# A norm between fp32 matmul stages taken in two token halves, and the units of the next stage rounded at other places

## The reference, cut to what matters

```python
def rmsnorm_2(x, g):
    xf = x.astype(jnp.float32)
    y = xf * lax.rsqrt(jnp.mean(xf * xf, axis=-1, keepdims=True) + EPS)
    return (y * g.astype(jnp.float32)).astype(x.dtype)
...
def hybrid_layer(h, p_i, pos, lb, norm_g, w_in, w_out, ffn1_gu, ffn1_down, ffn2_gu, ffn2_down,
                 hg_norm_g, sinks, sg_ln_g, sg_w, sg_b, ple_proj, ple_gate):
...
    h = h + 0.5 * rmsnorm_2(swiglu(rmsnorm_2(h, norm_g[0]), ffn1_gu, ffn1_down), norm_g[1])
    z = rmsnorm_2(h, norm_g[2]) @ w_in
...
    h = h + rmsnorm_2(mixed, norm_g[3])
    h = h + 0.5 * rmsnorm_2(swiglu(rmsnorm_2(h, norm_g[4]), ffn2_gu, ffn2_down), norm_g[5])
    gate = jax.nn.sigmoid(rmsnorm_2(h, norm_g[6]) @ ple_gate)
    h = h + rmsnorm_2((p_i @ ple_proj) * gate, norm_g[7])
    return h
```

## Time and profile before

| | us |
|---|---|
| median of three runs | 2706.15 (2705.19 to 2709.1) |
| the profiled execution | 2708.01, its span 2706.2 |
| PE busy | 2607.4 (96% of the span) |
| DVE busy | 1133.2 (42%) |
| ACT busy | 997.6 (37%) |
| POOL busy | 1261.9 (47%) |

### The profile page before, as it was taken

How to read it: one execution, slowest core, us unless ns; L and a number is a source line. 1 busy time by engine, 2 the same in 40 slices (tenths; PEclk the granted TensorE clock), 3 DMA queues, 4 the chain that set the end, 5 groups by cost and what they waited for, 6 DMA issues and landing times.

```text
span 2706.2 us, 33653 instructions
## 1 busy us (share of the span) xinstructions
PE 2607.4 (96%) x12436; PEld 2097.1 (77%) x12436; DVE 1133.2 (42%) x1712; ACT 997.6 (37%) x1482; POOL 1261.9 (47%) x1632
## 2 busy tenths in 40 slices
PE   6999999999999999999999999999999989999997
PEld 3788777787888877677888877888877767888875
DVE  5588666535221058625221046222018655222025
ACT  5233423524223244444323245323234454232234
POOL 1233467555555454135555455555544314555543
PEclk8999999999999999999999999999999999999999
DMA  6212211132333332112333322333322202333332
GB/s 269 70 55 71 79 46 40 54 118 86 101 95 94 100 92 67 35 56 85 96 99 93 102 93 80 100 94 96 99 86 84 63 24 86 93 95 100 95 96 74
DMA packets 63815, 234.24 MB, mean 87 GB/s; under 512 B 7361, under 2 KB 8001, under 8 KB 63169
## 3 DMA queue, kind: packets, MB, share of 16 engines
q1 hardware_dynamic: 61056, 222.33, 26.4%
q10 hardware_dynamic: 2624, 10.00, 1.0%
HBM read 230.00 MB, written 2.10 MB: 86 GB/s over the span
## 4 chain that ended last, share of the span: by engine, by line
PE 85%; DVE 9%; issue 3%; ACT 2%; POOL 1%; DMA 1%; SPq 0%; DVEq 0%; POOLq 0%; ACTq 0%
PE banks L1874 21%; PE banks L1864 21%; PE banks L1865 21%; PE banks L2215 2%; PE banks L2221 2%; PE banks L2216 2%; DVE tmp L1136 2%; DVE sq_sum L1115 1%; DVE xlo L1143 1%; PE banks L1934 1%; PE banks L2024 1%; PE banks L2336 1%; DVE h L1139 1%; PE banks L2285 1%; PE banks L2287 1%
## 5 line engine op out<-in xcount | busy, mean ns | idle before, releaser
L437 POOL TENSOR_TENSOR wlo<-raw,whi 128x256 fp32r<-128x256 f32 x1584 | 1181.8, 779 | 1371.9 <-ACT whi L528 1371.7
L1864 PE MATMUL banks<-xhi,whi 128*128 128x512 f32 x1920 | 752.5, 392 | 2.3 <-DVE z L1772 2.3
L1865 PE MATMUL banks<-xhi,wlo 128*128 128x512 f32 x1920 | 747.5, 389 | 0.0
L1874 PE MATMUL banks<-xlo,whi 128*128 128x512 f32 x1952 | 736.5, 393 | 10.2 <-DVE xlo L1143 10.1
L528 ACT ACTIVATE whi<-raw 128x1024 fp32r<-128x1024 f32 x396 | 415.1, 1053 | 348.3 <-PE banks L1874 337.8
L1874 PEld LDWEIGHTS banks<-xlo,whi 128*128 128x128 f32 x1952 | 365.8, 189 | 96.7 <-DVE xlo L1143 18.4
L1864 PEld LDWEIGHTS banks<-xhi,whi 128*128 128x128 f32 x1920 | 360.4, 188 | 82.0 <-DVE z L1772 3.1
L1865 PEld LDWEIGHTS banks<-xhi,wlo 128*128 128x128 f32 x1920 | 360.5, 188 | 76.5 <-issue 1.9
L1115 DVE TENSOR_TENSOR sq_sum<-sq_sum,tmp 128x512 f32<-128x512 f32 x110 | 85.3, 775 | 464.6 <-ACT tmp L548 464.6
L1864 PE MATMUL banks<-act_hi,whi 128*128 128x512 f32 x704 | 273.9, 389 | 0.0
L1865 PE MATMUL banks<-act_hi,wlo 128*128 128x512 f32 x704 | 273.9, 389 | 0.0
(11 more groups left out here) (419 smaller groups left out, 3186.8 us busy)
## 6 DMA issues: line engine op xcount, KB each, us to landing
raw<-in_stream SPq DMA_DIRECT2D x396, 512.0 KB, 3.5
ada_raw<-in_stream SPq DMA_DIRECT2D x24, 512.0 KB, 7.0
h<-in_x ACTq DMA_DIRECT2D x2, 2048.0 KB, 12.1
out<-h SPq DMA_DIRECT2D x4, 512.0 KB, 2.6
ctx_raw<-in_ctx ACTq DMA_DIRECT2D x1, 1024.0 KB, 19.6
dft_t<-in_dft_t ACTq DMA_DIRECT2D x1, 1024.0 KB, 4.8
ple_raw<-in_ple ACTq DMA_DIRECT2D x2, 512.0 KB, 3.5
mixpar<-in_mixpar ACTq DMA_DIRECT2D x2, 384.0 KB, 4.4
```

Of the source, the lines that this page charges most:

```text
L437: piece = pool.tensor_tensor(wlo[:, i, s], raw[:, i, s], whi[:, i, s].bitcast(F32), ALU.subtract)
L1864: pe.matmul(acc[acc_of[t]][:], whi[:, u % SLOTS, i], x_h, start=(k == 0), stop=False, skip_group_check=split)
L1865: pe.matmul(acc[acc_of[t]][:], wlo[:, u % SLOTS, i], x_h, start=False, stop=False, skip_group_check=split)
L1874: mm = pe.matmul(acc[acc_of[t]][:], whi[:, u % SLOTS, i], x_l, start=False, stop=(k == k_tiles - 1), skip_group_check=leading and m < leads)
```

## The change

The last tile of out1, down and out2 is computed for the tokens 0 to 255 (half A) and then for 256 to 511 (half B), in two banks (`last_tile`, `second`), with matmuls of 256 columns. The sum of the squares of the first seven tiles stands before the last k of half A, the sum of the last tile's squares of half A before k = 3 of half B, that of half B after the first eight matmuls of the next stage. The leading tiles take k = 0 to 3 (`AHEAD` = 4) for half A, then for half B, then k = 4 to 7 whole (`leading`). ACT and DVE follow the same order: norm, residual, high and low parts of k = 0 to 3 in halves. ACT's units of the next stage are rounded at other places, and more of them by the end of the boundary (`norm_in`, `y_out`). The sum of h's squares moves out of the leading tiles: to the start of tile 5, in in2 to k = 2 of tile 4. DVE's additions of h's squares all move behind k = 4, the last four to the end. After proj both halves of the inverse come first (`at_once`) and the last tile is whole; the last boundary of all is in halves for k < 4 too. A weight unit of a split last tile is released by half B. The load of `ple_raw` moves from before to after `norm_in`.

In all 680 matmuls of 512 columns become 1360 of 256: 48 in out1, 66 in each of four downs, 24 in each of two out2s, and 40 in each of eight leading groups.

The diff, cut:

```diff
+AHEAD = 4
...
+                bank.append(0 if m == n - 1 else m % 4)
...
+            if (name == "out1" or name[0] in ("down", "out2")) and m == n - 1:
+                second[t] = 1 if name == "out1" else bank[t - 1]
+                earlier_second[t] = last[second[t]]
+                last[second[t]] = t
...
+            def norm_in(q, gain):
+
+                at_once = q[1] == 0 and q[0]
+                last_square(0)
+                if at_once:
+                    last_square(1)
+                last_inverse(0)
+                if at_once:
+                    last_inverse(1)
+                high_parts(units_to(q) + 1)
                 for e in range(2):
-                    dst = inv_rms[:, e * HALF:e * HALF + HALF]
-                    act.wait_ge(*after("summed", (key, e)))
-                    act.activation(dst, bank[4 + e][:, 0:HALF], ACT.Ln, scale=1.0 / D, bias=eps).then_inc(*done("log", (key, e)))
-                    act.wait_ge(*after("log", (key, e)))
-                    act.activation(dst, dst, ACT.Exp, scale=-0.5).then_inc(*done("inverse", (key, e)))
-
-            def norm_in(q, gain):
-
-                high_parts(units_to(q) + SLOTS - 1)
-                for k in range(KT):
-                    if k == 2:
+                    if e and not at_once:
+                        last_square(1)
+                        high_parts(units_to(q) + SLOTS)
+                        last_inverse(1)
+                    for k in range(AHEAD):
+                        act.wait_ge(*after("h_new", (q, k, e)))
+                        act.activation(xhi[:, k, half(e)], h[:, k, half(e)], ACT.Copy, scale=gain[:, k:k + 1])\
+                            .then_inc(*done("x_high", (q, k, e)))
+                        if e == 0 and k == 1:
+                            high_parts(units_to(q) + SLOTS - 1)
+                if last_copy:
+                    last_copy.pop()()
+                for k in range(AHEAD, KT):
+                    if k == AHEAD:
                         high_parts(units_to(q) + SLOTS)
                     if k == 5:
                         high_parts(units_to(q) + SLOTS + 1)
+                    if k == KT - 1:
+                        high_parts(units_to(q) + SLOTS + 2)
+                    act.wait_ge(*after("h_new", (q, k)))
+                    act.activation(xhi[:, k], h[:, k], ACT.Copy, scale=gain[:, k:k + 1])\
+                        .then_inc(*done("x_high", (q, k)))
+                    squares("h_sq", q, k - AHEAD, h[:, k - AHEAD])
+                for k in range(KT - AHEAD, KT):
                     squares("h_sq", q, k, h[:, k])
...
-                for m in range(KT):
+                for m in range(KT - 1):
+                    if m == KT - 2:
+                        high_parts(first_block[stage] // UNIT + KT * k // UNIT + (stage[0] == "out2"))
                     tile_ready(stage, m, k)
                     t = first_tile[stage] + m
                     squares("y_sq", q, m, acc[acc_of[t]][:])
-                    if m < KT - 1:
+                    act.activation(y[:, m], acc[acc_of[t]][:], ACT.Copy).then_inc(*done("y_copied", (q, m), bank_of=t))
+                t = first_tile[stage] + KT - 1
+                if stage[0] == "out2":
+                    high_parts(first_block[stage] // UNIT + KT * k // UNIT + 2)
...
+                for e in range(2):
+                    v.wait_ge(*after("inverse", (post, e)))
+                    for k in range(AHEAD):
+                        renewed(k, half(e), (q_pre, k - 1, e) if k else None, [(q_pre, k, e)] + [(q_pre, k)] * e)
+                        if e == 0 and k == AHEAD - 1 and between:
+                            between()
+                        if k and q_pre != "last":
+                            lower(k - 1, half(e), (q_pre, k - 1, e))
+                    if q_pre != "last":
+                        lower(AHEAD - 1, half(e), (q_pre, AHEAD - 1, e))
+                for k in range(AHEAD, KT + 1):
+                    if k < KT:
+                        renewed(k, slice(0, SEQ), (q_pre, k - 1), [(q_pre, k)])
+                    if k > AHEAD and q_pre != "last":
+                        lower(k - 1, slice(0, SEQ), (q_pre, k - 1))
+                        sq_add("h_sq", q_pre, k - 1 - AHEAD)
+                for k in range(KT - AHEAD, KT) if q_pre != "last" else []:
+                    sq_add("h_sq", q_pre, k)
...
+                m, t = KT - 1, first_tile[stage] + KT - 1
+                for e in range(2):
+                    freed = earlier_second[t] if e else earlier[t]
+                    if counted and freed is not None:
+                        pe.wait_ge(*bank_free(freed))
+                    for k in range(k_tiles):
+                        if e == 0 and k == k_tiles - 1:
+                            first_squares()
+                        if e and k == when:
+                            sum_half(0)
+                        u, i = place(stage, m, k, k_tiles, leads)
+                        if e == 0 and (i == 0 or k == 0):
+                            pe.wait_ge(unit_split, u + 1 - WHOLE_UNITS)
+                        dst, w_h, w_l = last_half(t, e), whi[:, u % SLOTS, i], wlo[:, u % SLOTS, i]
+                        pe.matmul(dst, w_h, hi(k)[:, half(e)], start=(k == 0), stop=False)
+                        pe.matmul(dst, w_l, hi(k)[:, half(e)], start=False, stop=False)
+                        mm = pe.matmul(dst, w_h, lo(k)[:, half(e)], start=False, stop=(k == k_tiles - 1))
+                        keys = [("unit", u)] * (e and i == UNIT - 1) + [(stage, m, e)] * (k == k_tiles - 1)
+                        if keys:
+                            mm.then_inc(*done("product", *keys))
...
+            def leading(stage, key, sum_half):
+
+
+                for e in range(2):
+                    for k in range(AHEAD):
+                        leading_high(stage, key, k, e)
+                        if e == 0 and k == 0 and sum_half:
+                            sum_half(1)
+                        if k:
+                            leading_low(stage, key, k - 1, e)
+                    leading_low(stage, key, AHEAD - 1, e)
+                for k in range(AHEAD, KT):
+                    leading_high(stage, key, k)
+                    if k > AHEAD:
+                        leading_low(stage, key, k - 1)
+                leading_low(stage, key, KT - 1)
+
+            def tile_of(stage, m, k_tiles, leads, hi, lo, waits=None, amid=None):
+
...
+                    stage = (("gu", layer, 0), ("in2", layer), ("gu", layer, 1), ("gate", layer))[s]
+                    leading(stage, lambda k: (q, k), sum_half)
+                    amid = ((LEADS, 2) if s == 1 else (LEADS + 1, 0)), lambda: pre_sum(q)
+                    y_squares = lambda: first_squares("y_sq", q)
+                    sum_half = lambda e, q=q: last_squares(("post", q), "y_sq", q, e)
...
```

316 lines of the change are left out of this document (175 added, 141 removed).

## The result

The changed kernel takes 2720.26 us (median, 2718.26 to 2722.16), the kernel before beside it 2706.73: a ratio of 1.0044 with an interval of 1.0032 to 1.0056. It is **slower by some 12 us** by that ratio (the two medians lie 13.5 apart), more than twice the forecast's 4.6. Put on the forecast's 2706.15 the ratio gives 2718.1, just inside the 2697 to 2719 of the forecast; the bare median is 1.3 above it. The spans of the two profiled executions, 2706.2 and 2718.3, differ by 12.1, so the traces hold the whole difference.

The account below looks back on a forecast made before the run. PE, busy 2607.4 of 2706.2 us, was taken as the bound, with DVE pacing the leading tiles. Terms -4.0 + 3.4 + 2.0 - 0.2 + 2.0 + 1.4 = +4.6 us on 2706.15 gave 2710.8; range 2697 to 2719.

Parts of the forecast that it names:

- The price of a half: On PE, 0.1192 us per 256-column matmul, 0.0117 us more per split; down's last tile to leading tiles 17.0 us, -2.1.
- the leading tiles after down: From the first leading matmul to tile 4 after down: floor 22.8 us plus waits, 25.0 against 26.3, so -1.4.
- 0.9 for the half sum: Leading tiles after down: half B's square stands behind four copies and two units on ACT, so PE waits 0.9 us.
- The vector engine sets the pace: Leading tiles before the change: DVE, busy 25.48 of 26.30 us, sets their pace, and ACT's inverse sets their start.
- Down to in2: Two boundaries: PE's 3.5 us lead turns into waiting and z comes 1.7 us later each, +3.4 in all.
- The prediction's own sign: In in2, PE's wait for z should grow from 1.1 to 6 us, as a sign in the trace after.
- The late units: Units late for PE: 0.6 us twice at gate, 1.5 at three gu, 0.6 after proj, 6.3 in all.
- the units have slack: Rival, 28%: POOL may finish units before PE asks, and z needn't be later; faster, 2701 or 2697 us.
- The clock rival: Rival, 18%: TensorE's lower clock costs 1.6 us per PE-bound leading stage; three to five make 2715.5 to 2719 us.
- Proj to gu: One boundary, start and pace unchanged: moved sum 0.9, unit behind it 0.6, 40 splits 0.5, so +2.0 us.
- out2 to gu: Two boundaries: start 1.6 us earlier, leading tiles +0.2 with PE blocked 2.75, then later costs; +1.0 each, +2.0.
- the end: Last boundary, no matmul left to hide DVE: halves for k = 0 to 3 cost 7.8 instead of 6.4 us, +1.4.

Follow-up runs that it names:

- the last run: Changed kernel with half B's square and inverse earlier, last boundary whole, in2's clears behind z, gu's and gate's sum of h's squares at k = 4 of tile 4: 2703.24 us.

## Why the forecast was right in sign and short in size

- **The price of a half** held: seventeen microseconds from the last tile to the leading tiles were forecast, 17.1 measured; out1's start came 3.3 us earlier (3.2). That the split itself is paid (0.012 us each, not 0.0025) is in these numbers.
- **The step that was sized wrong is the leading tiles after down.** I set waits of 2.2 us there, 25.0 in all. They took 26.2 into in2 and 26.4 into gate, as long as before. The term "0.9 for the half sum" was 1.9, since DVE's half A was priced without POOL (5.5 us) although ACT's list puts two units right under it; it took 8.9, and 6.3 with the units cut short; after out2, where no unit lies under it, it took the 5.5. I had counted that collision for in2's end, but only behind the inverse of half B. The wait alone isn't the loss: with it gone, but the inverse of half B left late, tile 4 came 0.3 to 0.45 earlier, and with the collision gone 2.2 to 2.5. So tile 4 of gate, counted from down's last tile, was 1.95 us earlier than before, not 3.5.
- **"The vector engine sets the pace"** was read from a busy share, 25.48 of 26.30 us. PE's own waits for low parts in that stretch, two rows of its timeline before, came to 1.9 us, no more. There was less to gain from half A's early start than a share of 97% suggests.

```profile
987.76 1.21 PE L1874 MATMUL banks<-xlo,whi 128*128 128x512 f32 x4 [0.86 <-DVE xlo L1143]
...
997.64 1.19 PE L1874 MATMUL banks<-xlo,whi 128*128 128x512 f32 x4 [1.08 <-DVE xlo L1143]
```

- **Down to in2**: the mechanism held (PE's lead turned into waiting, z later), the term was 3.1 instead of 1.7, and it is as long as DVE's later end, 3.2 us. The prediction's own sign was set too high: PE's wait for z grew from 1.1 to 4.1 and not to 6. PE's lead was short by 1.3, and the moved sum (0.9) with its wait for the additions of squares (0.9, not in the forecast) used up 1.8 of it. From the inverse of half B on DVE needed 23.9 us (980.49 to 1004.40), and 23.8 were forecast; that inverse was the step, 21.7 us after the start of down's last tile instead of 20.4. It is late for the same cause as PE's half sum: the copies of half A, at the pace of a slowed DVE. That is 1.3 of the 1.4 us by which the term was short.
- **The late units** behind h's inverse were priced at 0.6 (gate) and 1.5 (gu); the last run shows 1.1 and 1.3. The rival "the units have slack" is refuted: they have none once h's inverse comes with the sum in tile 5.
- **The clock rival** had a part that can be seen and isn't large. Into gate PE ran its first seventeen halves after the wait at the lower level (0.21 us for 0.12, 1.5 us in all), into in2 it didn't and waited 1.0 for a unit instead; the leading tiles came out alike, +0.05 and -0.16. By the run with the clears moved, that is 0.2 us at each gate. At the two gu after out2 the granted clock was 0.94 as well, and no run has the same order at 1.00, so its share there stays open. What else stayed of the clock is attention's +0.95.

```profile
1591.28 0.85 PE L2059 MATMUL banks<-tmp,table 128*128 128x256 f32 x2 [1.76 <-ACT tmp L565]
...
1592.36 0.41 PE L1969 MATMUL banks<-xhi,whi 128*128 128x256 f32 x1
1592.57 0.41 PE L1970 MATMUL banks<-xhi,wlo 128*128 128x256 f32 x1
```

- **Proj to gu, out2 to gu and the end** were within 0.6, 0.4 and 0.05 us each. After proj that is luck in part: the leading tiles were 0.8 shorter where 0.5 more for the splits was forecast, and the tiles behind cost 2.2 instead of 1.5. After out2 I had put two units among ACT's copies of half A, where the trace has none; the wait was 2.5 instead of 2.75.

What stays open is how much of the 3.1 us at in2 the additions of squares at the end cost alone; no run moved them there with the rest in place. And whether half A after down can be had without the collision, with the first two units split before it as they are after out2, wasn't tried.

## What to carry to other kernels

When work is cut in halves so that the next stage can start early, follow both halves through every queue: here, after down, the first half's early start was paid back because the second half's square and inverse stood behind the first half's copies on ACT, and those went at the pace of a DVE that two units on POOL had slowed. A sum moved to a later place still holds up all that waits for its result; 2.7 us earlier on PE was worth 1.1 to 1.3 at each of six boundaries and turned a kernel 0.14% slower than before into one 0.19% faster. And the longest wait in a list need not be the one to remove: taking 1.9 us off it moved the end by 0.4, until the inverse behind it moved as well.

## What the runs showed of the hardware

DVE and POOL slow each other. An operation of 256 columns with two inputs from SBUF took DVE 0.48 us alone and 0.96 beside `wlo<-raw,whi`; POOL's pieces took 0.87 us (6.96 for eight) beside it and 0.71 alone. With 7.0 us of POOL under it half A took DVE 8.9 us, with 1.7 us it took 6.3, with none 5.5. The Trainium skill, "SBUF — State Buffer", section "SBUF: two separate sides", has an exclusive lock by which the loser fully blocks; the six pieces less, 4.2 us at 0.71 each, would then be an estimate of 4.2 us on DVE, and 2.6 were measured. POOL lost 1.3 at the same time, but the two didn't simply take turns: between 972.54 and 977.81 DVE started an operation every 0.88 us and POOL a piece every 0.87, where one of each in a row (0.46 and 0.71 alone) would need 1.17.

PE's granted clock fell to the lower level behind a wait of 1.75 us at some gates and not at others of the same form (0.94 and 1.00 for the leading tiles, in one execution), and it was 1.00 at every gate of the six runs in which that wait was gone and no longer one had come in its place. With halves for k = 0 only, PE waited 3.4 us for a high part instead, and the granted clock into gate was 0.83. What the lower level costs depends on what PE waits for next. It was nothing at in2 of layer 0, where 32 matmuls took 3.63 us instead of 2.06 ahead of a z that was late anyway, 0.2 us at a gate where a wait of 0.95 for a unit took up the rest, and 1.1 to 1.3 us where no such wait followed.
